# Norm factors applied behind the matmuls, with the raw residual transposed by halves as it is added

## The reference

```python
for i in range(DEPTH):                                   # DEPTH = 2
    hn = rms_norm(h, attn_norm_w[i])
    h = h + token_mixers(hn, w_in[i], ...) # gated delta rule, windowed and stick-breaking heads, @ w_out[i]
    hn = rms_norm(h, ffn_norm_w[i])
    if i % 2 == 0:
        h = h + swiglu(hn, ffn_w1[j], ffn_w3[j], ffn_w2[j])          # width 2816
    else:
        h = h + moe_swiglu(hn, router_w[j], moe_w1[j], moe_w3[j], moe_w2[j])   # 8 experts, 2 per token
    gate = jax.nn.sigmoid(rms_norm(h, ple_norm_w[i]) @ ple_gate[i])
    h = h + (p[i] @ ple_proj[i]) * gate
return rms_norm(h, final_norm_w)

def rms_norm(x, w):
    y = xf * lax.rsqrt(jnp.mean(xf * xf, axis=-1, keepdims=True) + RMS_EPS)
    return (y * w.astype(F32)).astype(x.dtype)
```

## Time and profile before

| | |
|---|---|
| median of 3 runs | 1720.54 us (1720.02 to 1720.63) |
| the profiled execution | 1722.51 us, its span 1720.8 us |
| busy, share of the span | PE 95%, PEld 81%, DVE 75%, ACT 61%, POOL 8% |
| chain that ended last | PE 89%, DVE 4%, ACT 4%, POOL 1%, DMA 1%, issue 1% |
| mean granted TensorE clock | 0.974 |
| stretch of the expert rounds | 706 to 1640 us of the span |

### The profile page before, as it was taken

One profiled execution on the slowest core, in us unless ns is written; L12 is line 12 of the kernel. 1 busy time (PEld: TensorE's weight loads), 2 busy tenths in 40 slices (PEclk: granted clock), 3 DMA queues, 4 the chain that ended last, 5 costly groups with the idle time before them and its releaser, 6 DMA issues.

```text
span 1720.8 us, 23469 instructions
## 1 busy us (share of the span) xinstructions
PE 1635.3 (95%) x8812; PEld 1392.9 (81%) x8812; DVE 1296.5 (75%) x1214; ACT 1047.9 (61%) x1005; POOL 144.8 (8%) x131
## 2 busy tenths in 40 slices
PE   6999989999899986999999999999999999999986
PEld 6989789998798975788887887887878878877864
DVE  4976555556687666788888888888888888888964
ACT  5646243334574724667676767677777767676743
POOL 0134100000012511000000000001000000002000
PEclk9999899999999998999999999999999999999998
DMA  7440154545444012999999999999999999999970
GB/s 287 169 149 1 50 202 178 199 169 220 151 168 171 2 49 86 370 365 357 389 363 360 382 367 359 380 358 382 367 358 383 367 348 392 367 351 411 368 275 25
DMA packets 65713, 459.91 MB, mean 267 GB/s; under 512 B 7408, under 2 KB 7792, under 8 KB 11632
## 3 DMA queue, kind: packets, MB, share of 16 engines
q1 hardware_dynamic: 61904, 445.88, 67.9%
q0 software_dynamic: 3744, 13.13, 2.0%
HBM read 450.58 MB, written 8.40 MB: 267 GB/s over the span
## 4 chain that ended last, share of the span: by engine, by line
PE 89%; DVE 4%; ACT 4%; POOL 1%; DMA 1%; issue 1%; DVEq 0%; POOLq 0%; ACTq 0%; SPq 0%
PE ps L1717 26%; PE ps L1719 26%; PE ps L1718 26%; PE ps L1835 2%; DVE wlo L626 2%; PE ps L1844 2%; ACT whi L622 1%; PE ps L2090 1%; PE ps L1904 1%; ACT xh L1036 1%; PE ps L1833 1%; DMA raw<-in_experts 1%; PE ps L1705 1%; POOL work L747 1%; PE ps L1816 0%
## 5 line engine op out<-in xcount | busy, mean ns | idle before, releaser
L626 DVE TENSOR_TENSOR wlo<-raw,whi 128x2048 fp32r<-128x2048 f32 x421 | 944.8, 2289 | 114.9 <-ACT whi L622 114.6
L622 ACT CAST whi<-raw 128x2048 fp32r<-128x2048 f32 x421 | 782.7, 1916 | 59.3 <-DMA raw<-in_experts 58.9
L1717 PE MATMUL ps<-whi,xh 128*128 128x512 f32 (+3 forms) x1568 | 623.1, 397 | 31.9 <-DVE wlo L626 20.0
L1718 PE MATMUL ps<-wlo,xh 128*128 128x512 f32 (+3 forms) x1568 | 616.3, 393 | 0.0
L1719 PE MATMUL ps<-whi,xl 128*128 128x512 f32 (+3 forms) x1568 | 616.0, 393 | 0.0
L1717 PEld LDWEIGHTS ps<-whi,xh 128*128 128x128 f32 x1568 | 297.6, 190 | 101.2 <-DVE wlo L626 17.3
L1719 PEld LDWEIGHTS ps<-whi,xl 128*128 128x128 f32 x1568 | 297.4, 190 | 67.1
L1718 PEld LDWEIGHTS ps<-wlo,xh 128*128 128x128 f32 x1568 | 298.0, 190 | 64.3
L1717 PE MATMUL ps<-xh,whi 128*128 128x256 f32 x656 | 186.2, 284 | 0.0
L1719 PE MATMUL ps<-xh,wlo 128*128 128x256 f32 x656 | 184.7, 282 | 0.0
L1718 PE MATMUL ps<-xl,whi 128*128 128x256 f32 x656 | 184.7, 282 | 0.0
(11 more groups left out here) (275 smaller groups left out, 1304.8 us busy)
## 6 DMA issues: line engine op xcount, KB each, us to landing
raw<-in_experts SPq DMA_DIRECT2D x336, 1024.0 KB, 4.8
raw<-in_stream SPq DMA_DIRECT2D x85, 1024.0 KB, 4.9
y_rows<-work POOLq DMA_DIRECT2D x7, 512.0 KB, 5.2
y_rows<-work POOLq DMA_DIRECT2D x1, 2560.0 KB, 9.1
cst<-in_consts SPq DMA_DIRECT2D x1, 1383.5 KB, 13.6
h<-in_x SPq DMA_DIRECT2D x1, 1024.0 KB, 5.0
x_rows<-hn POOLq DMA_DIRECT2D x1, 1024.0 KB, 4.4
out<-work SPq DMA_DIRECT2D x2, 512.0 KB, 2.7
```

Source lines behind the costliest of these rows:

```text
L622: nc.scalar.copy(whi[:, n % RING, :], raw[:, n % RING, :]).then_inc(s_hi, 1)
L626: nc.vector.tensor_tensor(wlo[:, n % RING, :], raw[:, n % RING, :], whi[:, n % RING, :].bitcast(F32), ALU.subtract).then_inc(s_lo, 1)
L1717: pe.matmul(out, ah, bh, start=start, stop=False)
L1718: pe.matmul(out, ah, bl, start=False, stop=False)
```

## The change

The row factor is no longer applied to h. PE transposes h itself, so the transposes need no sum of squares, and they need only one half of the columns at a time: groups 0 and 1 (`EARLY`) hold columns 0 to 511, groups 2 and 3 (`LATE`) the rest. At sites 1 to 5 the early groups are placed among matmuls that PE has to do before the second half is added. The squares are taken in halves by ACT (`squares_of`), `rstd` has one more small operation on POOL, and the factor is applied to the outputs:

- where tokens are on the partitions, as `scale` of ACT's copy (`J`, the sigmoid), as an operand of DVE's addition (`Y2`) and on the router's logits;
- where tokens lie along the row (`I`, `H`), by a row `rrow` of 256 factors in all partitions: PE makes it with two matmuls (`row_of_rstd`), DVE copies it out, and DVE multiplies each output by it. All ten `channels` of a layer are now DVE's, and in the dense stage DVE multiplies ahead of ACT's silu.

```diff
-def norm_tiles(t, occ):
-    for c in range(4):
-        t.add(("T", occ, c), c, "av")
+def turn_tiles(t, occ, banks):
+
+    for c, bank in banks:
+        t.add(("T", occ, c), bank, "av")
+
+
+EARLY, LATE = (0, 1), (2, 3)
...
             def rstd(occ):
 
-                pool.wait_ge(s_sumsq, NB * (occ + 1))
-                nc.gpsimd.tensor_scalar(area("rs", 66, 2), area("rs", 64, 2), 1.0 / D, EPS, ALU.mult,
+                pool.wait_ge(s_sumsq, 2 * NB * (occ + 1))
+                nc.gpsimd.tensor_tensor(area("rs", 68, 2), area("rs", 64, 2), area("rs", 66, 2),
                                         ALU.add).then_inc(st.sem, st.up())
...
# ScalarE
+            def squares_of(occ, m, items=None):
+
                 for b in range(NB):
-                    residual_ready(act, occ, b, items)
-                    nc.scalar.activation(hn[:, b, :], h[:, b, :], ACT.Square,
-                                         accum_out=area("rs", 64 + b, 1)).then_inc(s_sumsq, 1)
+                    residual_ready(act, occ, b, m, items)
+                    nc.scalar.activation(hn[:, b, 512 * m:512 * m + 512], h[:, b, 512 * m:512 * m + 512], ACT.Square,
+                                         accum_out=area("rs", 64 + 2 * m + b, 1)).then_inc(s_sumsq, 1)
...
             def mixers(L):
-                norm(3 * L)
+                if L == 0:
+                    turned_residual(0, EARLY)
+                    split.behind(("T", 0, 3), most=1)
+                    turned_residual(0, LATE)
+                    squares_of(0, 0)
+                else:
+                    turned_residual(3, LATE)
+                squares_of(3 * L, 1)
                 split.behind(("T", 3 * L, 3))
...
-                split.behind(("WO", L, 1, 0))
+                squares_of(3 * L + 1, 0)
+                split.behind(("WO", L, 1, 0), most=1)
+                turned_residual(3 * L + 1, EARLY)
+                turned_residual(3 * L + 1, LATE)
+                squares_of(3 * L + 1, 1)
+                split.behind(("WO", L, 1, 1))
...
             for f in range(NF):
-                filled(act, ("H", f))
-                if f >= 2:
-                    drained(act, ("H", f - 2), "v")
-                nc.scalar.activation(ffs[f % 2], bank(("H", f), 0, T), ACT.Silu).then_inc(s_free["a"], 1)
+                act.wait_ge(s_ffa, f + 1)
+                nc.scalar.activation(ffs[f % 2], ffs[f % 2], ACT.Silu).then_inc(s_ffs, 1)
                 split.behind(("H", f))
...
# VectorE
+            def channels(L, t):
+                key = ("I", L, t)
+                filled(dve, key)
+                for c in (2 * t, 2 * t + 1):
+                    if c < CQ + CA:
+                        dst = xc[:, c, 3:3 + T] if c < CQ else att[:, c - CQ, :]
+                        ins = nc.vector.tensor_tensor(dst, bank(key, T * (c % 2), T), rrow, ALU.mult)
+                ins.then_inc(s_free["v"], 1)
+
             def convolved(L, t):
 
-                drained(dve, ("I", L, t), "a")
+                channels(L, t)
+                drained(dve, ("I", L, t), "v")
...
                 gates(L)
+                row_of_rstd(("RB", L))
                 for t in range(5):
                     convolved(L, t)
...
                     if m == 0:
-                        split.behind(("WO", L, 1, m))
+                        split.behind(("WO", L, 1, m), most=1)
+                    turned_residual(3 * L + 1, (EARLY, LATE)[m])
+                split.behind(("WO", L, 1, 1))
...
             for f in range(NF):
-                drained(dve, ("H", f), "a")
+                filled(dve, ("H", f))
+                nc.vector.tensor_tensor(ffs[f % 2], bank(("H", f), 0, T), rrow, ALU.mult).then_inc(s_ffa, 1)
+                split.behind(("H", f), most=1)
+                dve.wait_ge(s_ffs, f + 1)
                 if f >= 2:
                     dve.wait_ge(s_ffg, f - 1)
                 nc.vector.tensor_tensor(ffp[f % 2], ffs[f % 2], bank(("H", f), T, T), ALU.mult).then_inc(s_free["v"], 1)
...
# TensorE
+            def turned_residual(occ, which, items=None):
+                residual_ready(pe, occ, NB - 1, which[0] // 2, items)
+                for c in which:
                     opened(("T", occ, c), items)
-                    if c == 0:
-                        pe.wait_ge(s_hn["a"], occ + 1)
-                        pe.wait_ge(s_hn["v"], occ + 1)
                     for q in range(4):
                         k, b = 2 * c + q // 2, q % 2
-                        ins = pe.transpose(bank(("T", occ, c), P * q, P), hn[:, b, P * k:P * k + P], ident)
+                        ins = pe.transpose(bank(("T", occ, c), P * q, P), h[:, b, P * k:P * k + P], ident)
                     ins.then_inc(s_fill, 1)
+
+            def row_of_rstd(key, occ):
+
+                opened(key)
+                pe.wait_ge(s_rstd, occ + 1)
+                for b in range(NB):
+                    ins = pe.matmul(bank(key, P * b, P), area("rstd", b, 1).broadcast_to([P, P]), ident, start=True, stop=True)
+                ins.then_inc(s_fill, 1)
...
+                late = ((0, 1, 2), lambda: turned_residual(3 * L, LATE)) if L else None
+                token_major(0, DG + 2 * HG, ("T", 3 * L), late)
+                row_of_rstd(("RB", L), 3 * L)
...
-                both_blocks([("WO", L, b, 1) for b in range(NB)], ("WO", L, 1), 512)
+                both_blocks([("WO", L, b, 1) for b in range(NB)], ("WO", L, 1), 512,
+                            between=((1, 0, 0), lambda: turned_residual(3 * L + 1, EARLY)))
...
+            early, late = range(KC // 2), range(KC // 2, KC)
+            for f in range(2):
                 opened(("H", f))
                 ready(pe, ("w13", f))
+                for c in EARLY:
+                    drained(pe, ("T", 1, c), "v")
+                dense_up(f, 0, early)
+                if f == 0:
+                    turned_residual(1, LATE)
+            for c in LATE:
+                drained(pe, ("T", 1, c), "v")
+            for f in range(NF):
+                if f >= 2:
+                    opened(("H", f))
+                    ready(pe, ("w13", f))
+                    dense_up(f, 0, early)
+                dense_up(f, 0, late)
+                dense_up(f, 1, range(KC)).then_inc(s_fill, 1)
+                if f == 0:
+                    row_of_rstd(("RB", DEPTH), 1)
+                else:
                     dense_down(f - 1)
             dense_down(NF - 1)
```

More of the change, by code:

```diff
@@ L125, in add @@
         n[0] += 1
-    norm_tiles(t, 3 * L)
+    turn_tiles(t, 3 * L, [(c, (4, 5, 6, 7)[c]) for c in EARLY + LATE] if L == 0 else [(c, c) for c in LATE])
     for b in range(NB):
         add(("J", L, b, 0), "a")
+    add(("RB", L), "v")
     for c in range(5):
-        add(("I", L, c), "a")
+        add(("I", L, c), "v")
     add(("G", L), "v")
@@ L135, in mixer_tiles @@
     add(("I", L, 5), "v")
-    add(("I", L, 6), "a")
+    add(("I", L, 6), "v")
     for c in range(3):
@@ L141, in mixer_tiles @@
         add(("V", L, c), "a")
-    add(("I", L, 8), "a")
+    add(("I", L, 8), "v")
     add(("I", L, 9), "v")
@@ L174, in mixer_tiles @@
         add(("OT", L, c), "av")
-    for m in range(2):
-        for b in range(NB):
-            add(("WO", L, b, m), "v")
+    for b in range(NB):
+        add(("WO", L, b, 0), "v")
+    for c in EARLY:
+        add(("T", 3 * L + 1, c), "av")
+    for b in range(NB):
+        add(("WO", L, b, 1), "v")
+    for c in LATE:
+        add(("T", 3 * L + 1, c), "av")
 def ple_tiles(t, L):
@@ L182, in ple_tiles @@
         for b in range(NB):
-            t.add(("PP", L, b, m), 4 + 2 * m + b, "")
-    norm_tiles(t, 3 * L + 2)
+            t.add(("PP", L, b, m), 2 * m + b, "")
+        turn_tiles(t, 3 * L + 2, [(c, 4 + c) for c in (EARLY, LATE)[m]])
     for m in range(2):
         for b in range(NB):
+            t.add(("PG", L, b, m), 4 + 2 * m + b, "a")
+        for b in range(NB):
             t.drain(("PP", L, b, m), "v")
-    for m in range(2):
-        for b in range(NB):
-            t.add(("PG", L, b, m), 2 * m + b, "a")
+        if L == 0 and m == 0:
+            turn_tiles(t, 3, [(c, c) for c in EARLY])
 def gather_tiles(t, when):
@@ L233, in plan_tiles @@
     mixer_tiles(t, 1)
-    norm_tiles(t, 4)
     t.add(("LG",), 4, "a")
@@ L881, in mixers @@
                 nc.scalar.activation(area("lnp"), area("e1", 0, 12), ACT.Ln).then_inc(s_gln, 1)
-                def channels(t):
-                    filled(act, ("I", L, t))
-                    for c in (2 * t, 2 * t + 1):
-                        if c < CQ + CA:
-                            dst = xc[:, c, 3:3 + T] if c < CQ else att[:, c - CQ, :]
-                            ins = nc.scalar.copy(dst, bank(("I", L, t), T * (c % 2), T))
-                    ins.then_inc(s_free["a"], 1)
-                    split.behind(("I", L, t))
                 def silu(j):
@@ L898, in mixers @@
                 for t in range(5):
-                    channels(t)
+                    split.behind(("I", L, t))
```

(21 more changed lines are left out.)

170 lines of the change are left out of this document (91 added, 79 removed).

## The result

| | before | after |
|---|---|---|
| median | 1720.59 us (1720.02 to 1722.06, 4 runs) | 1740.73 us (1739.83 to 1742.07, 4 runs) |
| ratio to before | | 1.0117, 95% interval 1.0103 to 1.0131 |
| span of the profiled execution | 1720.8 us | 1738.1 us |
| mean granted clock | 0.974 | 0.968 |
| busy: PE, DVE, ACT | 95%, 75%, 61% | 95%, 75%, 60% |

The account below looks back on a forecast made before the run. PE's waits for the scaled residual and weight slots, 41 us of 1721, were taken as the bound. Terms summed to +8.5, plus 3 for the clock: 1734.0 profiled, 1732 median; own range 1726 to 1738, 8 in 10 1721 to 1741.

Parts of the forecast that it names:

- The forecast case: Whole kernel: queued slots and added DVE work cost more than the early transposes save, 1732 us; chance 0.63.
- Start: Kernel start: first slot split by 15.4 us, so `J` starts there instead of 19.12; 3.7 us gained.
- Convolution stage: Both layers: DVE, already full, gets multiplications and the row's copy, so `N2` waits; +2.5 us per layer, +5.0 in all.
- Into the dense stage: Site 1: PE waits 6.9 us for `w13` 1's late split, then for the longer chain before `dense_down(0)`; +4.4 us.
- Out of the dense stage: Group 21: only `dense_down(20)`, 2.8 us, covers the 6.2 us chain behind `H`; +3.4 us.
- Gate and next `J`: Sites 2 and 3: gaps around the gate's transposes close, layer 1's `J` gains 0; -1.1 us together.
- Router: Site 4: logits ready earlier, but three casts and three splits stand in front of their use; 0.
- +3: Clock at new pauses: one drop of some 3 us taken out of four unpriced pauses.
- the clock drops at every new pause: Rival, all four new pauses: 8.5 + 4 x 3.2 = 21 us, 1742 us; chance 0.12.
- only the entries bind: Rival: DVE's new work at `N2` and behind group 21 hides; 1720.6 us, no change; chance 0.12.
- DVE becomes the bound: Rival, dense stage: DVE's 8.35 of 8.48 us overruns, two-slot groups taking 9.5; 1738 us; chance 0.05.
- the residual's chain binds: Rival, `w13` 1 and `J`'s second slot: slots are split before PE arrives; faster, 1710 us; chance 0.08.

Follow-up runs that it names:

- e2_squares: Changed kernel with one DVE weight split, behind `I` 4, put behind the squares of q and k in both layers: 1733.96 us.
- e7_router: Changed kernel with ACT's logits copy and DVE's selection ahead of expert-weight casts and splits, one split then ahead of the gathered `xl`: 1736.66 us.
- b8_before_gate: Kernel before the change, with one of the last gate's four weight slots cast and split behind the last expert copies: 1713.83 us, ratio 0.9966.
- e10_filler: Changed kernel with idle matmuls nobody reads, 10 ahead of `dense_down(0)` and 14 ahead of `dense_down(21)`: 1736.21 us.
- e5_entries: Changed kernel with slot casts or splits moved at four places (site 1, squares before `N2`, dense groups, site 3): 1701.78 us, ratio 0.9906 to before.
- e9_all: Changed kernel with the edits of `e5_entries`, `e7_router` (without its split before gathered `xl`) and two last-gate slots earlier: 1690.29 us, ratio 0.9832 to before.

## Why the prediction was right in direction and too small

The forecast case came true with its mechanism at each place; 1740.7 lies 8.7 us above the predicted 1732 and inside the range.

- *Start*, -3.7: -4.1 at the first product, -4.8 by the end of `J`. The first slot's chain came as worked out to 0.4 us.
- *Convolution stage*, +5.0: waits of 2.20 and 2.14 us, 4.3. `e2_squares` shows the cause. The two multiplications take 0.74 us together, as the pair in the earlier trace rows. The Trainium skill, VectorE: DVE Perf Modes, "The DRAIN you can't avoid", has an operation start only when the one before has left the pipe, and these rows disagree. The prediction left out that the same section makes an exception, which fits them: an operation that is not held starts earlier.
- *Into the dense stage*, +4.4: from -2.1 at `WO` to +3.4 at `dense_down(0)`, 5.5. The pause was 6.6 us (6.9 forecast), the one for the chain 2.4 (2.3). The 1.1 more is the clock: behind the pause PE works at half speed for 5.5 us, which is 2.8 us lost where the forecast had 1.7.
- *Steady dense*, 0: 0.
- *Out of the dense stage*, +3.4: 3.43.
- *Gate and next `J`*, -1.1: -1.6, from 10.3 behind `dense_down(21)` (5.0, the wait of 3.4, 1.6 for its low clock, and 0.2) to 8.7 at `J`. The pause inside `J` was 5.48 us (5.8 forecast).
- *Router*, 0: from the last addition of `WO` to the first expert product 28.5 us against 28.8. That zero hid two things, logits earlier and the slots in front of them; `e7_router` shows 5.8 us of waits between them. The prediction saw the three casts and took the balance as the answer.

**The term that was mis-sized is the clock**, the "+3" for one drop out of four unpriced pauses. Three of the four pauses dropped it (ahead of `dense_down(0)`, behind group 21, `N2` of layer 1), though for 3.4 us each and so at 1.6 to 1.7 us instead of 3: 5.0 together. Two more drops stand in this pair of profiles at pauses that the change did not touch and the prediction did not count: ahead of `WO` in layer 1 (5.2 us of work took 7.6, so 2.4), and at the first expert product (1.5). Together 8.9. But the 3.9 us of the last two are not shown to be a cost of the change, since the clock falls there in `b8_before_gate` as well; how often it does so in the kernel before, two profiles cannot say.

Up to the expert rounds the ledger has 18.8. Without the clock's 8.9 that leaves 9.9, where the terms without the "+3" gave 8.5. The start gave 1.1 more than its term, the pause of site 1 took 1.1 more, and 1.2 lie between `N2` and `WO` of layer 1, where the changed kernel does nothing new: there the kernel before took 118.1 us in this profile and 119.3 in that of `b8_before_gate`. Behind the 48 products the difference shrinks again, by 1.9 in the rounds, grows by 0.4 behind them, and comes to the 17.3 of the spans. The medians differ by 20 and not 17 because the profiled execution of before was 1.9 us above its median, that of after 0.9 below.

So of the 8.7 us by which 1732 was too low, 2.0 are drops at the new pauses, 3.9 are drops that the kernel before can have too, and 2.8 come from where the two profiled executions lie about their medians; what the other terms missed cancels out. The rival "the clock drops at every new pause" had the right total, 1742, by luck: it counted four drops at 3.2, where three came at 1.7.

The Trainium skill, TensorE: Matmul & The Clock Gate, "HAM oscillation", has the clock fall again at each pause between bursts. Its pauses, of some 3 to 5 us, are longer than the new ones here, of 2.1 to 3.4 us, so the section alone did not make that rival the forecast, as the prediction has it. Here the clock fell at three of the four, and `e10_filler` shows for two of them that work in the pause prevents it. The row that spoke against it, a pause of 2.3 us ahead of `WO` with the clock at 1.00, turned out the exception: in layer 1 the clock falls there in each of the 13 other profiles of this study. Two rows, one of each kind, were too few to make a chance from.

Of the other rivals, "only the entries bind" fell with the waits at `N2` (2.20 and 2.14 us) and behind group 21 (3.43), and "DVE becomes the bound" with the period of 8.47 us. The slots were not in time, so "the residual's chain binds" did not come true. Nor was its price of 1710 us right: with the slots of sites 1 and 3 in time and the two other costs left in, an estimate from the runs is 1719 us (the 1701.8 of `e5_entries`, and back 5.8, 10.3 and the 1.3 by which its expectation has the edits overlap). With all slots put in time (`e9_all`) the same change gives 1690 us.

What stays open: which of two equal pauses costs the clock, how much of the 20 us it is, and how much of the last gate's and the router's gain the kernel before could have in full; only one slot of the gate was tried there.

## What to carry to other kernels

When a chain is taken off the critical path, list what else was waiting behind it in the same queues and move that first: here waits of 4.4 to 5.6 us for the scaled residual went away at sites 1, 3 and 4, and the casts and splits of the next weights, queued behind the new small operations, took all of it back and more. The place of such background operations in a queue was worth 3 to 11 us each time, and moving them needed no new work. A background operation does not belong between two steps of a chain only because the steady state covers it: here the first and the last turn of the loop had no such cover. And a zero that is the difference of two large terms is a place to improve.

## What the runs showed of the hardware

- A pause of 2.4 or 3.4 us on PE cost 1.6 to 1.8 us more than itself by the clock (`e10_filler` against the changed kernel), and matmuls whose result nobody reads took that part away.
- A pause of 2.2 us, at `N2` of layer 0, dropped the clock in 2 of the 8 profiles of programs that are alike up to there.
- The clock column can be wrong at the head of a trace. The changed kernel's record of the granted clock begins only at 19.2 us, and for what lies before it the column says 1.00, while matmuls of 396 columns come every 0.33 us until 19.2 and every 0.18 from there, which is the half level and the full one. In the second profile of the same kernel the record begins at 10.3 us and shows the half level from 13.7 to 20.6.
- ACT's table load of 1.28 us went ahead of a first operation that waits for h alone (at 0.84 us), but behind PE's transposes (at 8.02) when the first operation was the copy that waits for them.
